# Moving SBUF blocks and reordering the routing of a one-core two-block forward pass

## The chip, the cores and the metric

The kernel runs on one core of one Trainium2 chip. The metric is the device time of one execution in microseconds; lower is better. A run of three executions gives a median with its lowest and highest value.

## The reference, cut to what matters

256 tokens of 1024 features go through two blocks in float32. The first block has two layers. Each layer is a hybrid mixer and a feed-forward; that of layer 0 is dense, that of layer 1 has eight experts of which each token takes two:

```python
def moe_swiglu(h, router_w, w1, w3, w2):
    t = h.reshape(bsz * seq, d)
    logits = jnp.einsum('td,de->te', t, router_w).astype(jnp.float32)
    top_vals, top_idx = lax.top_k(logits, TOP_K)          # TOP_K = 2
    top_w = jax.nn.softmax(top_vals, axis=-1)
    gates = jnp.sum(jax.nn.one_hot(top_idx, N_EXPERTS) * top_w[..., None], axis=1)
    for e in range(N_EXPERTS):
        a, b = t @ w1[e], t @ w3[e]
        out = out + gates[:, e:e + 1] * ((jax.nn.silu(a) * b) @ w2[e])
...
def second_block(x, ...):
    for l in range(DEPTH):                                # DEPTH = 2
        x = x + 0.5 * rmsnorm(swiglu_ffn(rmsnorm(x, g1), w_gu, w_down), g2)
        x = x + rmsnorm(mixing_sublayer(rmsnorm(x, g3), ..., rel_bias), g4)
        x = x + 0.5 * rmsnorm(swiglu_ffn(rmsnorm(x, g5), w_gu, w_down), g6)
```

The attention inside `mixing_sublayer` adds a bias from a table of 32 buckets by distance (`rel_bias`). The kernel makes that table of distances once, during the first block.

## The kernel before, in words

**Weights.** All weights come in 591 slabs of 128 x 2048 float32 (1 MB), in the order of use, through a ring of three slots. SyncE loads each slab into `raw` in two halves; ScalarE rounds a half to fp32r in `whi` (line 301); VectorE writes the remainder to `wlo` (line 737); TensorE then takes the slab. ScalarE and VectorE run two slabs ahead of TensorE. A slot of `raw` is loaded again once VectorE has done with it.

**Products.** Each product is three matmuls, in `slab` (lines 1306 to 1308): high activations with `whi`, high activations with `wlo`, low activations with `whi`. The activation block of 128 x 128 is the stationary operand and 512 weight columns are the moving one. The split activations have names by stage: `XH`/`XL` for all mixers and the up half of the feed-forwards over all 256 tokens, `GH`/`GL` for their down half; `XEH`/`XEL` and `GH_`/`GL_` for the same halves of the experts, which take one tile of 128 gathered tokens.

**Memory.** `memory` allocates in the order of its lines, from 16.1 KiB of each partition on. Before: `raw` 16 to 40 KiB, `whi` 40 to 64, `wlo` 64 to 88, `X` 88 to 96, `XN` 96 to 104, `XH` 104 to 112, `XL` 112 to 120, then small tables (`ident`, `small`, `pcols`), `region_b` from 122 (in it `mcum` 122 to 128, `LFH` and `LFL` 141 to 145), and `region_z` from 148 (in it `GH` 148 to 170, `GL` 170 to 192; or `GH_` 148 to 159, `GL_` 159 to 170, `XEH` 176 to 180, `XEL` 180 to 184, `PT` 185 to 186, `YH` and `YL` 186 to 194).

**Around the routing.** Every engine has its own written program, and semaphores order them. After the second mixer (`m1.out`) TensorE transposes `X` (line 1338), ScalarE and VectorE split it into `XH` and `XL` (lines 313, 314, 754, 755). TensorE makes the table of distances into four PSUM banks (line 1599), ScalarE copies it to `RB` (line 545), and Pool writes it to DRAM and reads it back with each row shifted (lines 1843, 1847). Then come 64 small matmuls for the router's logits (line 1608), a chain of small steps on VectorE that picks two experts per token, each waited for by the next (`step`), five counting matmuls (lines 1615 to 1619), the slot of each token (`slots`, line 977), and the gather of expert 0's tokens (line 1542). Expert e is `up` with 22 slabs, then `down` with 11; between them the result of expert e - 1 is scattered (lines 1551, 1552) and added to `X` (line 993). All work after that runs in the same way for the second block.

Of the kernel before, what the change touches and what calls it, by code (L numbers as in the profile page):

```python
# [58 lines left out]
class Tiles:  # L59
# [54 lines left out]
    def memory(self):  # L114
        self.raw = self.sb("raw", [P, RING, SLAB])
        self.whi = self.sb("whi", [P, RING, SLAB], F32R)
        self.wlo = self.sb("wlo", [P, RING, SLAB], F32R)
# [34 lines left out]
        n = 9 * SEG  # L152
        z = self.overlays("region_z", n, [("Z", [P, n], F32)], [
            ("GH", [P, FT, S], F32R), ("GL", [P, FT, S], F32R),
            ("SG", [P, 3, NT, S], F32), ("GN", [P, 3, NT, S], F32),
        ], [
            ("GH_", [P, FT, P], F32R), ("GL_", [P, FT, P], F32R),
            ("SG_", [P, 3, S], F32), ("GN_", [P, 3, S], F32),
            ("XEH", [P, KT, P], F32R), ("XEL", [P, KT, P], F32R),
            ("PM", [P, NT, P], F32),  # L160
            ("PT", [P, S], F32R),
            ("YH", [P, D], F32R), ("YL", [P, D], F32R),
            ("GB", [P, D], F32), ("RW", [P, KT, NE], F32), ("RWH", [P, KT, NE], F32R), ("RWL", [P, KT, NE], F32R),
            ("iota_", [P, P], F32), ("iota", [P, P], F32), ("ltri", [P, 3, P], F32), ("mo", [P, 512], F32),
        ], [
            ("Z2", [P, 12 * NT * CW], F32),
            ("HP", [P, 2, 30 + S], F32), ("CA", [P, 2, S], F32), ("CB", [P, 2, S], F32),
            ("QT", [P, 2, S], F32), ("KTT", [P, 2, S], F32), ("QI", [P, 2, S], F32),
            ("LG", [P, 4, S], F32), ("SCO", [P, 2, S], F32), ("WRK", [P, 2, S], F32), ("m8", [P, 16], F32),
        ])  # L170
        self.Z, self.GH, self.GL, self.SG, self.GN, self.GH_, self.GL_ = (z[n] for n in ("Z", "GH", "GL", "SG", "GN", "GH_", "GL_"))
        self.SG_, self.GN_, self.XEH, self.XEL, self.PM, self.PT, self.YH = (z[n] for n in ("SG_", "GN_", "XEH", "XEL", "PM", "PT", "YH"))
        self.YL, self.GB, self.RW, self.RWH, self.RWL, self.iota_, self.iota = (z[n] for n in ("YL", "GB", "RW", "RWH", "RWL", "iota_", "iota"))
        self.ltri, self.mo, self.Z2, self.HP, self.CA, self.CB, self.QT = (z[n] for n in ("ltri", "mo", "Z2", "HP", "CA", "CB", "QT"))
        self.KTT, self.QI, self.LG, self.SCO, self.WRK, self.m8 = (z[n] for n in ("KTT", "QI", "LG", "SCO", "WRK", "m8"))
# [110 lines left out]
class Scalar(Engine):  # L286
# [195 lines left out]
    def up(self, T, tiles, norm=None):  # L482

        for g in range(FF_GROUPS):
            self.hi(2)
            if 0 < g < FF_GROUPS - 1:
                self.turn(T, g - 1, tiles)
            elif g:
                self.turn(T, g - 1, tiles)
            self.gate(T, g, tiles, norm)  # L490

# [232 lines left out]
class Vector(Engine):  # L724
# [297 lines left out]
    def first_max(self, src, m, onehot, RI):  # L1022

        dve, k = self.eng, self.k
        A, TM = k.hot(1), k.mo[:, 292:294]
# [5 lines left out]
        self.step(dve.tensor_tensor(onehot, A, bc(TM), ALU.is_equal))  # L1031

    def moe(self):
# [10 lines left out]
        dve.wait_ge(*k.at("e.iota_"))  # L1044
        dve.tensor_copy(k.iota[:], k.iota_[:].bitcast(I32))
        dve.wait_ge(*k.at("e.rw"))
        self.step(dve.tensor_copy(k.RWH[:], k.RW[:]))
        dve.tensor_tensor(k.RWL[:], k.RW[:], k.RWH[:], ALU.subtract).then_inc(*k.up("dve_step", "e.rws"))
        rbt = k.bias_tmp[0:REL_BUCKETS, 0:4]
        rbb = k.bias_tmp[0:REL_BUCKETS, 4 + 2 * S:4 + 4 * S].rearrange("p (h l) -> p h l", h=4)  # L1050
        dve.wait_ge(*k.at("rbt"))
        dve.tensor_copy(rbb, rbt.rearrange("p (h o) -> p h o", o=1).broadcast_to([REL_BUCKETS, 4, P])).then_inc(*k.up("dve_step", "rbb"))
        LG, A, B, OH1, OH2, SEL, _, RI = (k.hot(i) for i in range(8))
        M1, M2, _, W1, W2 = (mo[:, 288 + 2 * i:290 + 2 * i] for i in range(5))
        bc = lambda a: a.rearrange("p (t o) -> p t o", o=1).broadcast_to([P, NT, NE])
        POS = mo[:, 160:178].rearrange("p (t e) -> p t e", e=NE + 1)
        GATE = mo[:, 180:198].rearrange("p (t e) -> p t e", e=NE + 1)
        POS2 = mo[:, 200:218].rearrange("p (t e) -> p t e", e=NE + 1)
        CNT, FLAG = mo[:, 220:228], mo[:, 230:231].bitcast(I32)
        tt, ts = dve.tensor_tensor, dve.tensor_scalar  # L1060
        dve.wait_ge(*k.at("e.lg"))
        for t in range(NT):
            self.step(ts(LG[:, t, :], ps[:, 6, t * NE:(t + 1) * NE], rs[:, t:t + 1], None, ALU.mult))
        for t in range(NT):
            self.step(ts(RI[:, t, :], k.iota[:, 0:NE], -1.0, float(NE), ALU.mult, ALU.add))
        self.first_max(LG, M1, OH1, RI)
        self.step(dve.scalar_tensor_tensor(out=B, in0=OH1, scalar=-BIG, in1=LG, op0=ALU.mult, op1=ALU.add))
        self.first_max(B, M2, OH2, RI)
        self.step(tt(W2, M2, M1, ALU.subtract), "e.w2")
# [209 lines left out]
    def program(self):  # L1279
# [16 lines left out]
class Tensor(Engine):  # L1296
# [247 lines left out]

    def scatter(self, T, e, t):
# [24 lines left out]
    def experts(self, T, GATE):  # L1570
# [4 lines left out]
        for e in range(NE):  # L1575
# [4 lines left out]
            self.up(U, 1, None, (lambda: self.scatter(T, e - 1, 0)) if e else None)  # L1580
# [10 lines left out]
    def moe(self):  # L1591
# [3 lines left out]
        rbb = k.bias_tmp[0:REL_BUCKETS, 4 + 2 * S:4 + 4 * S].rearrange("p (h l) -> p h l", h=4)  # L1595
# [15 lines left out]
        SEL, GATE = k.hot(5), mo[:, 180:198].rearrange("p (t e) -> p t e", e=NE + 1)  # L1611
        o = ps[:, 7, :]
# [6 lines left out]
        pe.matmul(o[:, 2 * NE:3 * NE], k.ltri[:, 1, :], SEL[:, 1, :], start=False, stop=True).then_inc(*k.up("pe_prod", "e.cum"))  # L1619
        pe.wait_ge(*k.at("e.flag"))  # L1620
        self.experts("x", GATE)
# [184 lines left out]
class Pool(Engine):  # L1806


    def start(self):
# [7 lines left out]
        pool.dma_start(k.mask_load[:], k.a["level_masks"]).then_inc(*k.up("d_mask_load", "mask_load", 16))  # L1817

# [229 lines left out]
```

## Time and profile before

| | |
|---|---|
| median of 3 executions | 3109.59 us (3104.79 to 3114.94) |
| the profiled execution, its own time | 3106.7 us |
| its span | 3104.9 us |
| TensorE (PE) busy | 2898.1 us, 93% |
| VectorE (DVE) busy | 2062.2 us, 66% |
| ScalarE (ACT) busy | 1696.0 us, 55% |
| DMA | 633.63 MB, mean 204 GB/s |
| experts, about 994 to 1823 us | DMA share 0.92 to 0.95 in each 100 us |

The span is the part of the time between the first and the last instruction in the profile. A busy share is an average over stages; matmuls overlap, so their busy time counts the stream of them and not each one's length. The granted clock is the share of 2.4 GHz that TensorE was given in a stretch; 0.5 is 1.2 GHz.

### The profile page before, as it was taken

The numbers are of one execution on the slowest core, as the hardware profiler recorded it, in microseconds if no ns is written. First come the engines' busy times: TensorE is split into PE (matmuls) and PEld (weight loads), VectorE is DVE, ScalarE is ACT, GpSimd is POOL, SyncE is SP. The second block draws the span as 40 slices with busy tenths as digits, with TensorE's granted clock in tenths as the row PEclk, the third lists the DMA queues.
The fourth block names the chain that finished last, engine by engine and source line by source line (L and its number), as shares of the span: only waits on it lengthen the run. The fifth ranks groups of instructions, "written<-read, shape, count | busy, mean of one in ns | idle before, by whom it ended". The sixth has DMA issues, their size and how long they took to land.

```text
span 3104.9 us, 34324 instructions
## 1 busy us (share of the span) xinstructions
PE 2898.1 (93%) x13334; PEld 2376.6 (77%) x13334; DVE 2062.2 (66%) x2910; ACT 1696.0 (55%) x2271; POOL 32.9 (1%) x55
## 2 busy tenths in 40 slices
PE   8998899999887999999999989989899999898998
PEld 6887688788765878777877768877778788776786
DVE  5566655656664898889888955468655455587553
ACT  5645354555523777677767754455454444555543
POOL 0000000000001000000000000000000000000000
PEclk9998899999987999999999989999999999999999
DMA  6443455454333999999989965544455555444453
GB/s 220 149 135 114 132 178 188 155 166 140 122 128 112 350 349 333 323 333 345 330 318 344 343 234 183 187 143 153 146 170 185 170 189 187 144 162 149 157 186 112
DMA packets 173658, 633.63 MB, mean 204 GB/s; under 512 B 19521, under 2 KB 19521, under 8 KB 173489
## 3 DMA queue, kind: packets, MB, share of 16 engines
q1 hardware_dynamic: 170752, 621.88, 59.0%
q0 software_dynamic: 2736, 9.49, 0.9%
q8 instruction: 107, 1.75, 0.2%
q14 instruction: 63, 0.51, 0.0%
HBM read 629.20 MB, written 2.10 MB: 203 GB/s over the span
## 4 chain that ended last, share of the span: by engine, by line
PE 78%; DVE 12%; DMA 4%; ACT 4%; issue 1%; SPq 0%; DVEq 0%; ACTq 0%; POOLq 0%
PE ps L1306 24%; PE ps L1308 23%; PE ps L1307 23%; DVE wlo L737 4%; DMA raw<-in_W 4%; PE ps L1418 2%; DVE CA L1182 2%; ACT whi L301 1%; PE ps L1495 1%; PE ps L1542 1%; PE ps L1338 1%; PE ps L1405 0%; PE ps L1404 0%; DVE XN L905 0%; DVE Z L1269 0%
## 5 line engine op out<-in xcount | busy, mean ns | idle before, releaser
L737 DVE TENSOR_TENSOR wlo<-raw,whi 128x1024 fp32r<-128x1024 f32 x1182 | 1394.0, 1221 | 560.4 <-ACT whi L301 550.8
L301 ACT ACTIVATE whi<-raw 128x1024 fp32r<-128x1024 f32 x1182 | 1197.8, 1057 | 600.8 <-PE ps L1308 547.7
L1306 PE MATMUL ps<-whi,XH 128*128 128x512 f32 (+1 forms) x2192 | 873.4, 398 | 41.2 <-DVE XL L755 17.3
L1307 PE MATMUL ps<-wlo,XH 128*128 128x512 f32 (+1 forms) x2192 | 859.0, 392 | 0.0
L1308 PE MATMUL ps<-whi,XL 128*128 128x512 f32 (+1 forms) x2192 | 859.0, 392 | 0.0
L1306 PEld LDWEIGHTS ps<-whi,XH 128*128 128x128 f32 x2192 | 418.8, 191 | 134.9 <-DVE XL L755 21.8
L1308 PEld LDWEIGHTS ps<-whi,XL 128*128 128x128 f32 x2192 | 417.6, 191 | 87.5
L1307 PEld LDWEIGHTS ps<-wlo,XH 128*128 128x128 f32 x2192 | 418.9, 191 | 82.8 <-issue 0.5
L1306 PE MATMUL ps<-whi,XEH 128*128 128x512 f32 x704 | 284.2, 404 | 1.4 <-DVE XEL L986 1.4
L1308 PE MATMUL ps<-whi,XEL 128*128 128x512 f32 x704 | 278.4, 395 | 0.0
L1307 PE MATMUL ps<-wlo,XEH 128*128 128x512 f32 x704 | 278.0, 395 | 0.0
L1306 PE MATMUL ps<-whi,GH 128*128 128x512 f32 x440 | 174.9, 397 | 0.0
L1308 PE MATMUL ps<-whi,GL 128*128 128x512 f32 x440 | 174.0, 395 | 0.0
L1307 PE MATMUL ps<-wlo,GH 128*128 128x512 f32 x440 | 174.0, 395 | 0.0
L1306 PE MATMUL ps<-whi,GH_ 128*128 128x512 f32 x352 | 147.8, 420 | 16.5 <-DVE X L993 16.5
L1308 PEld LDWEIGHTS ps<-whi,XEL 128*128 128x128 f32 x704 | 132.2, 188 | 31.6
L1306 PEld LDWEIGHTS ps<-whi,XEH 128*128 128x128 f32 x704 | 132.4, 188 | 30.0 <-DVE XEL L986 1.6
L1307 PEld LDWEIGHTS ps<-wlo,XEH 128*128 128x128 f32 x704 | 132.5, 188 | 28.7
L480 ACT ACTIVATE GH<-ps 128x512 fp32r<-128x512 f32 x55 | 32.9, 598 | 207.5 <-PE ps L1495 207.5
L943 DVE TENSOR_TENSOR GL<-ps,GH 128x512 fp32r<-128x512 f32 x55 | 38.0, 691 | 162.9 <-ACT GH L480 162.9
L1307 PE MATMUL ps<-wlo,GH_ 128*128 128x512 f32 x352 | 141.0, 400 | 0.0
L1308 PE MATMUL ps<-whi,GL_ 128*128 128x512 f32 x352 | 140.8, 400 | 0.0
(358 smaller groups left out, 2467.9 us busy)
## 6 DMA issues: line engine op xcount, KB each, us to landing
raw<-in_W SPq DMA_DIRECT2D x1182, 512.0 KB, 5.2
GP<-in_ffn_post_g POOLq DMA_DIRECT2D x4, 512.0 KB, 4.0
X<-in_x SPq DMA_DIRECT2D x1, 1024.0 KB, 5.0
skew<-RB POOLq DMA_DIRECT2D x4, 256.0 KB, 2.8
RB<-skew POOLq DMA_DIRECT2D x8, 128.0 KB, 2.5
GP<-in_mix_post_g POOLq DMA_DIRECT2D x2, 512.0 KB, 3.8
out<-X SPq DMA_DIRECT2D x1, 1024.0 KB, 4.0
mload<-in_cum_sums POOLq DMA_DIRECT2D x1, 768.0 KB, 8.5
```

The lines of the kernel that those rows point to most:

```text
L301: act.activation(k.whi[:, slot, part], k.raw[:, slot, part], ACT.Copy).then_inc(*k.up("act_hi"))
L480: act.activation(GH[:, 2 * g:2 * g + 2, :], src, ACT.Copy).then_inc(*k.up("act_split", f"{T}.gh{g}"))
L737: dve.tensor_tensor(k.wlo[:, slot, part], k.raw[:, slot, part], k.whi[:, slot, part], ALU.subtract).then_inc(*k.up("dve_lo"))
L943: dve.tensor_tensor(GL[:, 2 * g:2 * g + 2, :], src, GH[:, 2 * g:2 * g + 2, :], ALU.subtract).then_inc(*k.up("dve_split", f"{T}.gl{g}"))
L1182: x = dve.scalar_tensor_tensor(out=CA[:, c, :], in0=HP[:, c, j:j + S], scalar=dw(c, j), in1=CA[:, c, :], op0=ALU.mult, op1=ALU.add)
L1306: pe.matmul(ps, xh, k.whi[:, slot, cols], start=first, stop=False)
L1307: pe.matmul(ps, xh, k.wlo[:, slot, cols], start=False, stop=False)
L1308: mm = pe.matmul(ps, xl, k.whi[:, slot, cols], start=False, stop=last)
L1338: mm = pe.transpose(bank[:, i * S + t * P:i * S + (t + 1) * P], src(2 * b + i, t), k.ident[:])
L1418: mm = pe.matmul(o, x, x, start=True, stop=True)
L1495: mm = pe.transpose(turned[:, fb, t * P:(t + 1) * P], GN[:, t, fb * P:(fb + 1) * P], k.ident[:])
L1542: mm = pe.matmul(k.ps[:, 6 + c // 4, (c % 4) * P:(c % 4 + 1) * P], k.XN[:, t, c * P:(c + 1) * P], k.PM[:, t, :], start=t == 0, stop=t == N ...
```

## The change

Two things change. First the order of allocation. `wlo`, `ident`, `small`, `pcols` and the router's tables go to the end; `region_z` moves ahead of `region_b`. After: `raw` and `whi` as before, `X` 64 to 72 KiB, `XN` 72 to 80, `XH` 80 to 88, `XL` 88 to 96, `region_z` from 96 (`GH` 96 to 118, `GL` 118 to 140; `GH_` 96 to 107, `GL_` 107 to 118, `XEH` 124 to 128, `XEL` 128 to 132), `region_b` from 168, `wlo` 195 to 219.

Second the order of the routing. The router's tables are loaded at the start and prepared on VectorE behind the first mixer; the bias rows are copied behind the second mixer; the table of distances is made by TensorE and copied by ScalarE after the first two slabs of expert 0; the gates are worked out after the slots; two comparisons become one instruction each; the counts go to bank 5 and the unused ninth column of the slot tables goes away.

```diff
     def memory(self):
         self.raw = self.sb("raw", [P, RING, SLAB])
         self.whi = self.sb("whi", [P, RING, SLAB], F32R)
-        self.wlo = self.sb("wlo", [P, RING, SLAB], F32R)
         self.X = self.sb("X", [P, NT, D])
         self.XN = self.sb("XN", [P, NT, D])
         self.XH = self.sb("XH", [P, KT, S], F32R)
         self.XL = self.sb("XL", [P, KT, S], F32R)
-        self.ident = self.sb("ident", [P, P])
-        self.small = self.sb("small", [P, 192])
-        self.pcols = self.sb("pcols", [P, PCOLS])
-
+        n = 9 * SEG
+        z = self.overlays("region_z", n, [("Z", [P, n], F32)], [
...
         b = self.overlays("region_b", 6816, [
...
+        self.wlo = self.sb("wlo", [P, RING, SLAB], F32R)
+        self.ident = self.sb("ident", [P, P])
+        self.small = self.sb("small", [P, 192])
+        self.pcols = self.sb("pcols", [P, PCOLS])
...
+    def distances(self):
+        act, k = self.eng, self.k
+        act.wait_ge(*k.at("dist"))
+        act.activation(k.RB[:].rearrange("p t h l -> p (t h l)").rearrange("p (h l) -> p h l", h=4), k.ps[:, 4:8, :], ACT.Copy).then_inc(*k.up("act_step", "distc"))
+
...
-            self.up(U, 1)
+            self.up(U, 1, None, self.distances if U == "x.e0" else None)
...
     def moe(self):
         act, k = self.eng, self.k
         self.norm_in("e.n", lambda i: k.pcols[:, LCOLS + 8 + i:LCOLS + 9 + i])
-        act.wait_ge(*k.at("dist"))
-        act.activation(k.RB[:].rearrange("p t h l -> p (t h l)").rearrange("p (h l) -> p h l", h=4), k.ps[:, 4:8, :], ACT.Copy).then_inc(*k.up("act_step", "distc"))
         W2 = k.mo[:, 296:298]
...
+    def router_tables(self):
+        dve, k = self.eng, self.k
+        dve.wait_ge(*k.at("e.iota_"))
+        self.step(dve.tensor_copy(k.iota[:], k.iota_[:].bitcast(I32)))
+        dve.tensor_scalar(k.small[:, 144:152], k.iota[:, 0:NE], -1.0, float(NE), ALU.mult, ALU.add).then_inc(*k.up("dve_step"))
+        dve.wait_ge(*k.at("e.rw"))
+        self.step(dve.tensor_copy(k.RWH[:], k.RW[:]))
+        dve.tensor_tensor(k.RWL[:], k.RW[:], k.RWH[:], ALU.subtract).then_inc(*k.up("dve_step", "e.rws"))
...
-        self.step(dve.tensor_tensor(A, src, bc(m), ALU.is_equal))
-        self.step(dve.tensor_tensor(A, A, RI, ALU.mult))
+        for t in range(NT):
+            x = dve.scalar_tensor_tensor(out=A[:, t, :], in0=src[:, t, :], scalar=m[:, t:t + 1], in1=RI, op0=ALU.is_equal, op1=ALU.mult)
+        self.step(x)
...
         self.lo(LEAD)
         self.mixer1(0)
+        self.router_tables()
         self.ffn1()
         self.mixer1(1)
+        self.bias_rows()
         self.moe()
...
-            self.up(U, 1, None, (lambda: self.scatter(T, e - 1, 0)) if e else None)
+            self.up(U, 1, None, (lambda: self.scatter(T, e - 1, 0)) if e else self.distances if U == "x.e0" else None)
+            if U == "x.e0":
+                pe.wait_ge(*k.at("distc"))
...
+    def distances(self):
+        pe, k = self.eng, self.k
+        rbb = k.bias_tmp[0:REL_BUCKETS, 4 + 2 * S:4 + 4 * S].rearrange("p (h l) -> p h l", h=4)
+        pe.wait_ge(*k.at("rbb"))
+        pe.wait_ge(*k.at("hot"))
+        pe.wait_ge(*k.at("e.flag"))
+        for h in range(4):
+            mm = pe.matmul(k.ps[:, 4 + h, :], rbb[:, h, :], k.bias_tmp[0:REL_BUCKETS, 4:4 + 2 * S], start=True, stop=True)
+        mm.then_inc(*k.up("pe_prod", "dist"))
...
         self.norm_in("e.n", ["m1.out"])
-        rbb = k.bias_tmp[0:REL_BUCKETS, 4 + 2 * S:4 + 4 * S].rearrange("p (h l) -> p h l", h=4)
-        pe.wait_ge(*k.at("rbb"))
-        pe.wait_ge(*k.at("hot"))
-        for h in range(4):
-            mm = pe.matmul(ps[:, 4 + h, :], rbb[:, h, :], k.bias_tmp[0:REL_BUCKETS, 4:4 + 2 * S], start=True, stop=True)
-        mm.then_inc(*k.up("pe_prod", "dist"))
         pe.wait_ge(*k.at("e.n3.l"))
         pe.wait_ge(*k.at("e.rws"))
-        pe.wait_ge(*k.at("distc"))
```

TensorE's program behind the second mixer, before (`RWH` and `RWL` are the router's split weights, `bias_tmp` the rows of the table):

```order
L1308 MATMUL ps<-whi,XL 128x512
L1338 MATMUL ps<-ident,X 128x128 x16
L1599 MATMUL ps<-bias_tmp 128x512 x4
L1608 MATMUL ps<-RWH,XH 128x8
L1608 MATMUL ps<-RWL,XH 128x8
```

and after:

```order
L1323 MATMUL ps<-whi,XL 128x512
L1353 MATMUL ps<-ident,X 128x128 x16
L1630 MATMUL ps<-RWH,XH 128x8
L1630 MATMUL ps<-RWL,XH 128x8
L1630 MATMUL ps<-RWH,XL 128x8
```

The table's matmuls no longer stand between the transposes and the logits. They stand in expert 0 now, after its first two slabs:

```order
L1321 MATMUL ps<-whi,XEH 128x512
L1322 MATMUL ps<-wlo,XEH 128x512
L1323 MATMUL ps<-whi,XEL 128x512
L1569 MATMUL ps<-bias_tmp 128x512 x4
L1321 MATMUL ps<-whi,XEH 128x512
```

Here a slab's matmuls stand on both sides of them. VectorE's program from the second choice to the slots, before (`mo` holds all small routing values, `PM` the slots):

```order
L1069 TENSOR_TENSOR mo<-mo 128x2
L1071 TENSOR_SCALAR mo<-mo 128x2
L1072 RECIPROCAL mo<-mo 128x2
L1073 TENSOR_TENSOR mo<-mo 128x2
L1074 MEMSET mo 128x60
L1075 TENSOR_TENSOR mo<-mo 128x16
L1076 TENSOR_TENSOR mo<-mo 128x16
L1077 TENSOR_TENSOR mo<-mo 128x2x8
L1078 TENSOR_TENSOR mo<-mo 128x16
L1080 TENSOR_SCALAR mo<-ps 128x16
```

and after:

```order
L1079 TENSOR_TENSOR mo<-mo 128x16
L1080 TENSOR_TENSOR mo<-mo 128x2
L1083 SCALAR_TENSOR_TENSOR XN<-X,small,GB 128x1024 x2
L1086 TENSOR_SCALAR mo<-ps 128x16
L1087 TENSOR_TENSOR mo<-mo 128x16
L1088 TENSOR_SCALAR mo<-mo 128x16
L979 TENSOR_SCALAR PM<-iota,mo 128x128 x2
L1091 TENSOR_SCALAR mo<-mo 128x2
L1092 RECIPROCAL mo<-mo 128x2
```

The sum of the two choices (1078, now 1079), for which the counting matmuls wait, stands first; `XN` stands between it and the step that reads the counts; the gates stand behind the slots.

## Rows read from the trace of the kernel before

**Rows 1.** The page's head.
```profile
span 3104.9 us, 34324 instructions
```
**Rows 2.** The chain of waits around the routing: start, length, work.
```profile
951.38 2.48 DVE XN L1042 x2
...
954.74 7.21 PE ps L1599 x8
961.97 1.89 ACT RB L545
963.99 13.80 PE ps L1608 x64
...
983.17 0.60 PE ps L1615 x2
...
987.64 5.36 PE ps L1542 x32
...
994.40 0.50 PE ps L1306
```
**Rows 3.** TensorE's timeline, steady work of feed-forward 0: start, length, instruction.
```profile
480.08 0.39 PE L1306 MATMUL ps<-whi,XH 128*128 128x512 f32 x1
...
489.38 0.40 PE L1308 MATMUL ps<-whi,XL 128*128 128x512 f32 x1
...
555.16 0.40 PE L1306 MATMUL ps<-whi,GH 128*128 128x512 f32 x1
...
564.96 0.40 PE L1306 MATMUL ps<-whi,GH 128*128 128x512 f32 x1
```
**Rows 4.** VectorE's timeline in the routing.
```profile
948.07 0.47 DVE L755 SCALAR_TENSOR_TENSOR XL<-ps,pcols,XH 128x256 fp32r<-128x256 f32 x1
...
977.82 0.49 DVE L1063 TENSOR_SCALAR mo<-ps,small 128x8 f32<-128x8 f32 x2 [23.13 <-PE ps L1608]
...
982.94 0.17 DVE L1078 TENSOR_TENSOR mo<-mo 128x16 f32<-128x16 f32 x1
```
**Rows 5.** Stretches: length, busy us, then granted clock, DMA share, GB/s.
```profile
948.00:954.00 6.00, 0.00 (x0) 0.00 (x0) 3.32 (x7) 3.12 (x6) 0.00 (x0) 0.66 0.00 0
...
962.00:978.00 16.00, 13.79 (x64) 13.73 (x64) 0.18 (x1) 3.13 (x2) 6.41 (x12) 0.50 0.42 132
...
480.00:565.00 85.00, 85.00 (x379) 69.24 (x378) 42.02 (x44) 35.62 (x43) 0.00 (x0) 1.00 0.57 187
```
**Rows 6.** VectorE's timeline behind the first mixer.
```profile
386.54 0.48 DVE L754 SCALAR_TENSOR_TENSOR XL<-ps,pcols,XH 128x256 fp32r<-128x256 f32 x1 [1.62 <-ACT XH L314]
```
**Rows 7.** DMA issues of the table, 900 to 1060 us: size, us to landing.
```profile
skew<-RB POOLq DMA_DIRECT2D x4, 256.0 KB, 2.8
RB<-skew POOLq DMA_DIRECT2D x8, 128.0 KB, 2.5
```
**Rows 8.** Stretches inside the experts; columns as in rows 5.
```profile
1010.00:1040.00 30.00, 30.00 (x136) 24.16 (x135) 27.89 (x32) 24.41 (x32) 0.00 (x0) 1.00 1.00 364
...
1080.00:1180.00 100.00, 98.34 (x452) 79.71 (x452) 88.41 (x94) 74.02 (x91) 0.00 (x0) 1.00 0.95 336
```
**Rows 9.** TensorE's timeline, decay sums and a scatter.
```profile
103.27 0.39 PE L1404 MATMUL ps<-mcum,LFH 128*128 128x512 f32 x1
...
105.13 0.40 PE L1306 MATMUL ps<-whi,XH 128*128 128x512 f32 x1
...
1099.57 0.40 PE L1551 MATMUL ps<-YH,PT 128*128 128x512 f32 x1
...
1100.48 0.40 PE L1306 MATMUL ps<-whi,XEH 128*128 128x512 f32 x1
```
**Rows 10.** Groups of instructions on the page: busy, mean ns, idle before.
```profile
L301 ACT ACTIVATE whi<-raw 128x1024 fp32r<-128x1024 f32 x1182 | 1197.8, 1057 | 600.8 <-PE ps L1308 547.7
...
L1307 PE MATMUL ps<-wlo,XH 128*128 128x512 f32 (+1 forms) x2192 | 859.0, 392 | 0.0
...
L1306 PE MATMUL ps<-whi,GH_ 128*128 128x512 f32 x352 | 147.8, 420 | 16.5 <-DVE X L993 16.5
```

More of the change, by code:

```diff
@@ L121, in memory @@
         self.XL = self.sb("XL", [P, KT, S], F32R)
-        self.ident = self.sb("ident", [P, P])
-        self.small = self.sb("small", [P, 192])
-        self.pcols = self.sb("pcols", [P, PCOLS])
+        n = 9 * SEG
+        z = self.overlays("region_z", n, [("Z", [P, n], F32)], [
+            ("GH", [P, FT, S], F32R), ("GL", [P, FT, S], F32R),
+            ("SG", [P, 3, NT, S], F32), ("GN", [P, 3, NT, S], F32),
+        ], [
+            ("GH_", [P, FT, P], F32R), ("GL_", [P, FT, P], F32R),
+            ("SG_", [P, 3, S], F32), ("GN_", [P, 3, S], F32),
+            ("XEH", [P, KT, P], F32R), ("XEL", [P, KT, P], F32R),
+            ("PM", [P, NT, P], F32),
+            ("PT", [P, S], F32R),
+            ("YH", [P, D], F32R), ("YL", [P, D], F32R),
+            ("GB", [P, D], F32), ("mo", [P, 512], F32),
+        ], [
+            ("Z2", [P, 12 * NT * CW], F32),
+            ("HP", [P, 2, 30 + S], F32), ("CA", [P, 2, S], F32), ("CB", [P, 2, S], F32),
+            ("QT", [P, 2, S], F32), ("KTT", [P, 2, S], F32), ("QI", [P, 2, S], F32),
+            ("LG", [P, 4, S], F32), ("SCO", [P, 2, S], F32), ("WRK", [P, 2, S], F32), ("m8", [P, 16], F32),
+        ])
+        self.Z, self.GH, self.GL, self.SG, self.GN, self.GH_, self.GL_ = (z[n] for n in ("Z", "GH", "GL", "SG", "GN", "GH_", "GL_"))
+        self.SG_, self.GN_, self.XEH, self.XEL, self.PM, self.PT, self.YH = (z[n] for n in ("SG_", "GN_", "XEH", "XEL", "PM", "PT", "YH"))
+        self.YL, self.GB, self.mo, self.Z2, self.HP, self.CA, self.CB, self.QT = (z[n] for n in ("YL", "GB", "mo", "Z2", "HP", "CA", "CB", "QT"))
+        self.KTT, self.QI, self.LG, self.SCO, self.WRK, self.m8 = (z[n] for n in ("KTT", "QI", "LG", "SCO", "WRK", "m8"))
         b = self.overlays("region_b", 6816, [
@@ L150, in memory @@
         self.gvb, self.ones, self.ones1, self.mask_load, self.GP, self.bias_tmp = (b[n] for n in ("gvb", "ones", "ones1", "mask_load", "GP", "bias_tmp"))
[L152 to L174, printed above, removed]
@@ L175, in memory @@
-        self.KTT, self.QI, self.LG, self.SCO, self.WRK, self.m8 = (z[n] for n in ("KTT", "QI", "LG", "SCO", "WRK", "m8"))
+        self.wlo = self.sb("wlo", [P, RING, SLAB], F32R)
+        self.ident = self.sb("ident", [P, P])
+        self.small = self.sb("small", [P, 192])
+        self.pcols = self.sb("pcols", [P, PCOLS])
+        self.RW, self.RWH, self.RWL = self.sb("RW", [P, KT, NE]), self.sb("RWH", [P, KT, NE], F32R), self.sb("RWL", [P, KT, NE], F32R)
+        self.iota_, self.iota, self.ltri = self.sb("iota_", [P, P]), self.sb("iota", [P, P]), self.sb("ltri", [P, 3, P])
@@ L480, in turn, with up @@
         act.activation(GH[:, 2 * g:2 * g + 2, :], src, ACT.Copy).then_inc(*k.up("act_split", f"{T}.gh{g}"))
-    def up(self, T, tiles, norm=None):
+    def up(self, T, tiles, norm=None, after_first=None):
         for g in range(FF_GROUPS):
             self.hi(2)
-            if 0 < g < FF_GROUPS - 1:
-                self.turn(T, g - 1, tiles)
-            elif g:
+            if g:
                 self.turn(T, g - 1, tiles)
             self.gate(T, g, tiles, norm)
+            if g == 0 and after_first:
+                after_first()
     def down(self, T, tiles, between=None):
@@ L1038, in moe @@
         self.norm_in("e.n", lambda i: k.pcols[:, LCOLS + 8 + i:LCOLS + 9 + i])
-        dve.wait_ge(*k.at("e.n.rs"))
+        LG, A, B, OH1, OH2, SEL = (k.hot(i) for i in range(6))
+        M1, M2, _, W1, W2 = (mo[:, 288 + 2 * i:290 + 2 * i] for i in range(5))
+        bc = lambda a: a.rearrange("p (t o) -> p t o", o=1).broadcast_to([P, NT, NE])
+        POS = mo[:, 160:176].rearrange("p (t e) -> p t e", e=NE)
+        GATE = mo[:, 180:196].rearrange("p (t e) -> p t e", e=NE)
+        POS2 = mo[:, 200:216].rearrange("p (t e) -> p t e", e=NE)
+        CNT, FLAG = mo[:, 220:228], mo[:, 230:231].bitcast(I32)
+        tt, ts = dve.tensor_tensor, dve.tensor_scalar
+        dve.wait_ge(*k.at("e.n.rs"))
+        dve.wait_ge(*k.at("e.lg"))
+        for t in range(NT):
+            x = ts(LG[:, t, :], ps[:, 6, t * NE:(t + 1) * NE], rs[:, t:t + 1], None, ALU.mult)
+        self.step(x)
+        self.first_max(LG, M1, OH1)
+        self.step(dve.scalar_tensor_tensor(out=B, in0=OH1, scalar=-BIG, in1=LG, op0=ALU.mult, op1=ALU.add))
+        self.first_max(B, M2, OH2)
+        self.step(tt(SEL, OH1, OH2, ALU.add), "e.sel")
+        self.step(tt(W2, M2, M1, ALU.subtract), "e.w2")
         dve.wait_ge(*k.at("e.gb"))
@@ L1043, in moe @@
         x.then_inc(*k.up("dve_step", "e.xn"))
[L1044 to L1049, printed above, removed]
-        rbb = k.bias_tmp[0:REL_BUCKETS, 4 + 2 * S:4 + 4 * S].rearrange("p (h l) -> p h l", h=4)
[L1051 to L1069, printed above, removed]
+        dve.wait_ge(*k.at("e.cum"))
+        self.step(ts(A, ps[:, 5, 0:16].rearrange("p (t e) -> p t e", t=NT), 1.0, None, ALU.add))
+        self.step(tt(A, A, SEL, ALU.mult))
+        self.step(ts(POS, A, -1.0, None, ALU.add))
+        self.slots("x", 0, POS)
         dve.wait_ge(*k.at("e.w2e"))
@@ L1619, in moe @@
         pe.matmul(o[:, 2 * NE:3 * NE], k.ltri[:, 1, :], SEL[:, 1, :], start=False, stop=True).then_inc(*k.up("pe_prod", "e.cum"))
+        self.experts("x", GATE)
         pe.wait_ge(*k.at("e.flag"))
-        self.experts("x", GATE)
         more = pe.value_load(mo[0:1, 230:231].bitcast(I32), min_val=0, max_val=1)
```

41 lines of the change are left out of this document (20 added, 21 removed).

## The prediction

> **What bounds the kernel now.** I read the page first, for the span of 3104.9 us [rows 1] and for who is busy, then stretches of it: in feed-forward 0 TensorE is busy 85.00 of 85 us [rows 5], in the experts 98.34 of 100 us [rows 8]. So the time is TensorE's own work and the few places where it stops. Then the chain of waits at the place that the diff touches. Between the second mixer's last output and the first expert's first weight slab lies a stretch with no weight work: transposes of X, the distance table at 954.74, its copy on ScalarE at 961.97, the router's 64 small matmuls at 963.99, the counting matmuls at 983.17, the gather at 987.64, the first slab at 994.40 [rows 2]. These are a chain, each step waiting for the one before, and the weight ring holds only three slabs, so the DMA stands still too. Third, the distance between starts of neighbouring matmuls in steady work. With stationary XH or XL it is (489.38 - 480.08) / 41 = 0.2268 us, with GH or GL it is (564.96 - 555.16) / 42 = 0.2333 us [rows 3]. Both are 512 columns at the full clock (1.00 from 480 to 565 [rows 5]) and share whi and wlo as moving operand. What differs is where the stationary block lies: XH and XL at 104 to 120 KiB, GH and GL at 148 to 192 KiB.
>
> **The change, part by part: the routing.** (a) The table leaves the way. Now the router's matmuls wait for its copy; later they wait only for XL, whose last piece starts at 948.07 and takes 0.47 [rows 4], so they can start at 948.54 instead of 963.99: 15.4 us less. XN, iota and the split of the router's weights also stood ahead of the table's product on VectorE, from 951.38 on; the split and iota are done long before in the new order, and XN comes later (d). (b) The 64 matmuls took 13.8 us at the half clock, 1.2 GHz: the granted clock was 0.66 between 948 and 954, where no matmul ran, and 0.50 from 962 to 978 [rows 5]. In the new order they start during that fall, so the first few may run at 2.4 GHz; if all did, half of 13.8, 6.9 us, would go. In their 13.8 us at 1.2 GHz they did not raise the clock, so I take 0.7. (c) VectorE's steps from the logits (977.82) to the sum of the two choices (its last step at 982.94, 0.17 long) are 5.3 us; a step costs about 0.2 [rows 4]. Up to that sum the new order has 14 instructions in 11 waited steps, hence 11 x 0.2 and three more of 0.17, 2.7 us: 2.6 less. (d) From there to the gather it was 987.64 - 983.11 = 4.5 us. The counting matmuls (2.4) stay. XN (2.48 for the pair [rows 2]) now runs beside them, with one small step ahead, and ends some 0.3 later than they do. Behind it stand three steps and the slot pair instead of seven and the pair: 3.9 us, 0.6 less. The gates follow while the gather runs (5.4 us against nine steps, 1.9). Sum: 15.4 + 0.7 + 2.6 + 0.6 = 19.3 us less; bounds 17 (the steps save less than I count) and 25.5 (all 64 matmuls at the full clock).
>
> The tables now made on VectorE right behind the first mixer are four short instructions, under 1 us; there it idled 1.62 us for ScalarE's first XH piece [rows 6]; the next step would be 1 us late only if that cover went. The 0.4 us copy of the bias rows stands in the same kind of gap behind the second mixer. Pool's loads move to the start, ahead of bias_tmp, which is wanted 900 us later. No cost.
>
> **The table inside expert 0.** TensorE does the same eight passes, 7.2 us at the half clock [rows 2], so 3.6 at the full one. The experts have no slack for them: there TensorE has 1.7 us of 100 to spare [rows 8]. ScalarE waits in line for the table and copies it (1.89 us) before it splits the next slab; two slabs are split ahead, 5.6 us of TensorE's work, against 1.9 + 2 x 1.06 [rows 10] and VectorE's half about as long again, 5.1, so that just fits. Behind the copy Pool writes four blocks of 256 KB and reads eight of 128 KB [rows 7], 2.1 MB. They ran in the idle stretch; now they meet the weights where the DMA share is 1.00 at 364 GB/s [rows 8]: 2.1 / 0.364 = 5.8 us of transfer. Bounds: 3.6 us (transfers hidden, TensorE being late anyway) and 3.6 + 5.8 = 9.4. The DMA runs just in time there and the two delays overlap, so I take 6.5.
>
> **The addresses.** As allocated, whi stays at 40 to 64 KiB. wlo goes from 64 to 88 up to 195 to 219, XH and XL from 104 to 120 down to 80 to 96. GH takes 96 to 118 and GL 118 to 140. In the experts GH_ and GL_ take 96 to 118, XEH 124 to 128, XEL 128 to 132 (before: 148 to 184). Nothing in the trace shows a wlo this high beside a low stationary block. The nearest rows: the scatter has both operands high (PT 185, YH and YL 186 to 194), and its starts lie (1100.48 - 1099.57) / 4 = 0.2275 apart [rows 9], as close as with both low. So a high stationary block alone is not what costs 7 ns; a pair of which one is low and one high is. The decay sums of the first mixer, with LFH and LFL at 141 to 145 and mcum at 122 to 128, go at (105.13 - 103.27) / 8 = 0.2325 [rows 9], which says that a boundary lies near 120 to 140, where GL and XEL will stand. By the pair reading, three matmuls (whi with XH, wlo with XH, whi with XL) take 0.680 now and 0.687 with wlo high.
> - XH and XL: 2192 such threes [rows 10] x 6.7 ns = 14.6 us more; TensorE waits for others in small parts of the mixers, so 13.
> - GH and GL: 5 feed-forwards x 11 slabs x 8 = 440 threes at 0.700. With half of GL beyond the boundary they come to about 0.687: 6 us less.
> - Experts: 704 threes with XEH and 352 with GH_, now 0.700 (the 352 are counted in rows 10; 8 experts x 22 slabs x 4 are the 704). XEL, high, is loaded while wlo, high, streams, so 20 ns less on the 704 and 13 on the 352: 18.8 us. But the DMA share there is already 0.95 at 336 GB/s [rows 8], and TensorE's waits for X before the down slabs (16.5 us in all [rows 10]) have VectorE behind them, queued for late slabs. I take half, 9; bounds 4 and 19.
>
> Where the rows give one number, the Trainium skill gives another: "SBUF — State Buffer", section "Who interferes with whom", says that TensorE never waits on anyone and names no address as slow. By it the address part is worth nothing, while rows 3 differ by 7 ns between blocks that differ in nothing else. I go by the rows; the rule's outcome is the third rival.
>
> **Sum**: -19.3 + 6.5 + 13 - 6 - 9 = -14.8 us. The profiled execution took 3106.7 us, so 3091.9; it lies 2.9 below the median of the three runs, 3109.6, and against that median the forecast is 3094.8, rounded to 3095.
>
> **Rivals.** (1) Only the stationary address counts, wlo's does not. For it: every slow three above has a high stationary block, and I have just one kind of row with both high. Against it: that row. Then XH and XL cost nothing, GH and GL save 7 us, the experts 704 x 13.3 ns + 352 x 20 ns = 16.4 us, of which 9 come through: -19.3 + 6.5 - 7 - 9 = -29, 3081. (2) The slower side: wlo high costs at both changes, from whi to wlo and from wlo back, 13.3 ns per XH three. For it: a switch to a far moving operand is not shown free anywhere. That is 29 us, 26 of them felt; GH keeps 2 and the experts 4, so +26 - 6 - 12.8 = +7, 3117. It decides from about 8 ns per XH three on (12.8 + 6 = 18.8 us over 2192). (3) The addresses do nothing, the 7 ns has another cause, and only the routing is left: -19.3 + 6.5 = -12.8, 3097. For it: the page's rule; against it: rows 3.
>
> **Chances.** Forecast 0.40, (1) 0.30, (2) 0.15, (3) 0.15. A measurement here can tell about 0.3%, 9.3 us, from no change. The forecast's own range is 3082 to 3106, from routing 17 to 25, table 3.6 to 9.4 and experts 4 to 19. Faster than 3100.3: 0.8 of the forecast, all of (1), 0.75 of (3), 0.1 of (2), together 0.75; within the bound 0.15; slower 0.10. The range goes from (1) with more of the experts' gain and part of the clock's (3070) to (2) at 3117, cut at 3116.
>
> **What would show it.** The first router matmul at about 5 us behind the last X, still at or near the full clock; the gather's start 19 us earlier; the table's eight passes behind the first two slabs of expert 0 and the Pool transfers inside a stretch with DMA share 1.00. Then the starts in steady work: XH threes at 0.687 (forecast), 0.680 (rivals 1 and 3) or 0.693 (rival 2); GH threes at 0.687, or still 0.700 (rival 3). And experts that each take about 1 us less, expert 0 apart. The prediction is wrong if the XH threes stay at 0.680, which makes it faster, or if expert 0 loses more than the upper bound because the weights fall behind for good.

## The result: slower by 0.4%, not faster by 0.5%

Over 12 runs of each on the same chips the kernel before took 3112.89 us (median) and the changed one 3122.61 us: ratio 1.0038, 95% interval 1.0027 to 1.0049. The forecast was 3095 against 3109.6, a ratio of 0.9953; the time lies above the whole range, on the slower side. The profiled execution of the changed kernel took 3126.1 us against the 3106.7 us that the sum was made for: 19.4 more instead of 14.8 less. One execution each of two kernels below took 14.8 and 7.2 ms; it is in their medians and not in their ratios, which compare undisturbed executions alone.

The page of the changed kernel, its head and one group (columns as in [rows 10]):

```profile
span 3124.1 us, 34321 instructions
...
L1322 PE MATMUL ps<-wlo,XH 128*128 128x512 f32 (+1 forms) x2192 | 868.2, 396 | 0.0
```

Against [rows 10] the wlo-with-XH group's mean went from 392 to 396 ns. The matmuls' ends are modelled, so the distance between starts says more. TensorE's timeline of the changed kernel in the feed-forward of [rows 3]:

```profile
479.88 0.40 PE L1321 MATMUL ps<-whi,XH 128*128 128x512 f32 x1
...
481.98 0.40 PE L1321 MATMUL ps<-whi,XH 128*128 128x512 f32 x1
...
554.82 0.40 PE L1321 MATMUL ps<-whi,GH 128*128 128x512 f32 x1
...
560.42 0.40 PE L1321 MATMUL ps<-whi,GH 128*128 128x512 f32 x1
```

A "three" is the group of three matmuls that makes one product. Three threes with XH take 2.10 us, 0.700 each (0.680 before), and eight with GH 5.60, again 0.700. XH was to go to 0.687, GH down to 0.687.

The chain of waits around the routing (start, length, work), as [rows 2]:

```profile
952.41 1.24 DVE X L925
...
958.53 13.83 PE ps L1630 x64
972.46 0.37 DVE mo L1074 x2
...
975.50 2.48 DVE XN L1083 x2
978.52 0.49 DVE PM L979 x2
979.05 6.67 PE ps L1557 x32
...
987.12 0.50 PE ps L1321
...
992.94 3.64 PE ps L1569 x8
...
1007.05 9.85 DMA raw<-in_W
```

The router's matmuls (L1630) follow 4.9 us behind the last X and the gather (L1557) 25.4 behind it; before, the gather came 43.95 behind (987.64 against a last X that ended at 943.69). The table (L1569) has gone into expert 0, and behind it stands one long wait for a weight load.

With the ends of VectorE's X updates as marks (for expert 0 the first of its two), the difference of the two profiled executions (after minus before, us) splits so:

| stretch | before | after | difference | forecast |
|---|---|---|---|---|
| start to the end of mixer 2 | 943.7 | 953.6 | +9.9 | part of the +13 - 6 |
| to the first slab of expert 0 | 50.7 | 33.5 | -17.2 | -19.3 |
| to the X update of expert 0 | 108.2 | 115.1 | +6.9 | +6.5 |
| experts 1 to 7 | 722.5 | 728.4 | +6.0 | -9 |
| to the last X update of the kernel | 1275.4 | 1289.1 | +13.7 | rest of the +13 - 6 |

Routing and expert 0 did nearly what was forecast. Of the error of some 34 us, 32 are in the three rows of the addresses: +29.6 instead of -2. The other 2.5 are in the routing and expert 0.

### The profile page after: what moved, and what is told of

Read it like the earlier page. It is cut to its first block, busy times and chain, and to the rows that moved or that the text cites. A ratio compares the mean times of both kernels' runs of the same rounds, so it can differ in the third digit from the quotient of the medians.

```text
span 3124.1 us, 34321 instructions
## 1 busy us (share of the span) xinstructions
PE 2924.0 (94%) x13334; PEld 2376.5 (76%) x13334; DVE 2061.2 (66%) x2907; ACT 1696.2 (54%) x2271; POOL 33.4 (1%) x55
## 4 chain that ended last, share of the span: by engine, by line
PE 74%; DVE 14%; DMA 7%; ACT 4%; issue 1%; SPq 0%; DVEq 0%; ACTq 0%; POOLq 0%
PE ps L1321 22%; PE ps L1322 22%; PE ps L1323 22%; DMA raw<-in_W 7%; DVE wlo L739 7%; PE ps L1433 2%; DVE CA L1195 2%; ACT whi L300 1%; PE ps L1557 1%; PE ps L1510 1%; PE ps L1353 1%; PE ps L1420 0%; PE ps L1419 0%; DVE XN L907 0%; DVE Z L1282 0%
## 5 line engine op out<-in xcount | busy, mean ns | idle before, releaser
L1321 PE MATMUL ps<-whi,XH 128*128 128x512 f32 (+1 forms) x2192 | 883.9, 403 | 42.2 <-DVE XL L757 19.9
L1322 PE MATMUL ps<-wlo,XH 128*128 128x512 f32 (+1 forms) x2192 | 868.2, 396 | 0.0
```

Source lines behind the costliest of these rows:

```text
L1321: pe.matmul(ps, xh, k.whi[:, slot, cols], start=first, stop=False)
L1322: pe.matmul(ps, xh, k.wlo[:, slot, cols], start=False, stop=False)
```

## The experiments

In every kernel below the length of a three is the time from one matmul of whi with XH (or GH) to the next such matmul; the means are over all unbroken threes of the trace (1867 to 1875 with XH, 420 with GH).

**Routing alone, layout alone, wlo back, XH last.** The first keeps the old places with the new routing, the second the new places with the old routing. The third is the changed kernel with one tensor moved, the fourth the kernel before with XH and XL behind everything.

```diff
 # wlo third (from the changed kernel)
+        self.wlo = self.sb("wlo", [P, RING, SLAB], F32R)   # behind whi
-        self.wlo = self.sb("wlo", [P, RING, SLAB], F32R)   # behind region_b
 # XH last (from the kernel before): the two lines below go behind region_z
-        self.XH = self.sb("XH", [P, KT, S], F32R)
-        self.XL = self.sb("XL", [P, KT, S], F32R)
```

> The new order of the routing with the old places of all blocks (router tables added at the end). Theory A (the routing gains, the addresses lose): 10 to 13 us faster than before, since the changed kernel's stretch from the last X of the second mixer to expert 0's X add is 10.4 us shorter; XH threes stay at 0.680, GH threes at 0.700. Rival B (the moved table spoils the later experts for good): within 4 us of before, because what is gained ahead of expert 0 is lost again in experts 1 to 7.

Measured: 3093.39 us, ratio 0.9947 (0.9932 to 0.9962); XH 0.681, GH 0.700. That is 16 us, on the side of more than the 12.8 worked out.

> The new places of all blocks with the old order of the routing. Theory A: 20 to 25 us slower than before, with XH threes at 0.700 nearly everywhere and GH threes still at 0.700. Rival B: 8 to 12 us slower, all of the measured loss.

Measured: 3135.79 us, ratio 1.0083 (1.0067 to 1.0099), 26 us slower; XH 0.697, GH 0.700. So the layout alone costs more than the whole change, and costs it at XH.

> The changed kernel with wlo back in its old third place, all else behind it by 24 KiB (XH 104 to 112, XL 112 to 120, GH 120 to 142, GL 142 to 164). Theory A1 (a high wlo slows the threes): XH threes 0.680 again, 24 to 30 us faster than the changed kernel, so 10 to 15 faster than before; GH threes somewhere from 0.687 to 0.700. Rival A2 (XH and XL were worse at 80 to 96 KiB than at 104 to 120): the same here, to be told apart by a kernel with both low.

Measured: 3084.14 us, ratio 0.9915 (0.9892 to 0.9938); XH 0.6815, GH 0.681. One tensor's place is worth 1.0038 against 0.9915, about 38 us.

> The kernel before with XH and XL allocated last (204 to 220 KiB), wlo low. If a high stationary block beside low moving operands costs 20 ns a three, the XH threes come to 0.700 and the time to 25 to 40 us above before. If only wlo's place counts, XH threes stay at 0.680 and the time within 5 us.

Measured in one execution: 3146.02 us; XH and GH both 0.700. The XH threes of all four kernels can still be told by height: a pair of a low and a high operand is slow. But GH at 120 to 164 KiB in the third kernel gave 0.681, and GH at 132 to 176 in the fourth 0.700; height alone does not order these two. What does is the start address as a remainder. `pcols` takes 416 bytes (392, rounded up to a multiple of 32) and region_b 27,264, neither a multiple of 256, so whatever stands behind one of them is shifted. The blocks that a matmul reads lie multiples of 512 bytes behind the start of their tensor, so the start alone sets the remainder. From the allocation of each kernel, the start address modulo 256 bytes:

| kernel | whi | wlo | XH, XL | GH, GL | XH three | GH three |
|---|---|---|---|---|---|---|
| before; routing alone | 128 | 128 | 128 | 160 | 0.681 | 0.700 |
| changed; layout alone | 128 | 0 | 128 | 128 | 0.697 | 0.700 |
| wlo third | 128 | 128 | 128 | 128 | 0.6815 | 0.681 |
| XH last | 128 | 128 | 160 | 160 | 0.700 | 0.700 |

A three is at 0.680 where all its operands agree and near 0.700 where one does not. The scatter and the decay sums of [rows 9] fit as well: mcum leaves 32 and LFH 160 (0.2325 a matmul), PT, YH and YL all 160 (0.2275). This table was read off after the runs, so it had to be put to the test against height.

**High but agreeing; GH shifted in place.** The first is the changed kernel with wlo exchanged with region_b: wlo at 168.1 KiB, remainder 128. The second is the kernel before with 224 unused bytes.

```diff
 # wlo high and agreeing (from the changed kernel): wlo's line goes ahead of region_b
+        self.wlo = self.sb("wlo", [P, RING, SLAB], F32R)
         b = self.overlays("region_b", 6816, [
 # the kernel before, region_z shifted
+        self.sb("shift", [P, 56])
         n = 9 * SEG
         z = self.overlays("region_z", n, [("Z", [P, n], F32)], [
```

> The changed kernel with wlo exchanged with region_b: wlo still lies high, at 168.1 KiB behind region_z instead of 194.75, but its start address now leaves 128 modulo 512 bytes as whi, XH, XL and region_z do (256 before). Theory H, height (a low/high pair of operands is spaced wider): XH and XL stay low, so XH threes stay near 0.693 to 0.700 us and the time stays within 5 us of the changed kernel's, near 3120. Theory M, modulo (the spacing depends on whether the start addresses of the operands agree in their remainder): XH threes 0.680, GH threes 0.680, the time near that of the kernel with wlo back in third place, ratio 0.991 to 0.993 to the kernel before, some 30 us under the changed kernel.

Measured: 3083.14 us, ratio 0.9907 (0.9887 to 0.9927); XH 0.681, GH 0.681. TensorE's timeline of that kernel:

```profile
481.46 0.39 PE L1321 MATMUL ps<-whi,XH 128*128 128x512 f32 x1
...
486.90 0.39 PE L1321 MATMUL ps<-whi,XH 128*128 128x512 f32 x1
```

Eight threes in 5.44 us, 0.680 each, with wlo still 88 KiB above XH. Height is out as the cause.

> The kernel before with 224 unused bytes ahead of region_z and nothing else: GH and GL stay at 148.6 and 170.6 KiB, but their remainder modulo 512 goes from 416 to 128, that of whi and wlo. Theory H, height: GH threes stay at 0.700 us, ratio 1.000. Theory M, modulo: GH threes 0.680, some 450 threes by 0.020 us = 9 us, ratio 0.997; XH threes 0.680 by both. Experts 1 to 7 stay at 725 to 730 us by both if their bound is the transfers.

Measured: 3094.26 us, ratio 0.9953 (0.9936 to 0.9971); GH 0.6805. Its timeline where [rows 3] have 0.2333 a matmul:

```profile
554.24 0.39 PE L1307 MATMUL ps<-whi,GH 128*128 128x512 f32 x1
...
559.68 0.39 PE L1307 MATMUL ps<-whi,GH 128*128 128x512 f32 x1
```

5.44 / 8 = 0.680. 224 bytes that nobody uses made the kernel before about 14.6 us faster. In the profiled executions, 18.3 us apart, the five feed-forwards are 1.0 to 1.6 us shorter each, 7.0 together, where 9 were worked out from the threes; the four mixers, parts of which use region_z too, give 6.4, routing with expert 0 1.2 and the other experts 3.7. What the mixers gave was not forecast and not taken apart.

**Which differences cost.** The kernel before with 8 or 32 floats of padding ahead of XH and padding ahead of region_z.

```diff
+        self.sb("shx", [P, 8])      # 32 in the second kernel
         self.XH = self.sb("XH", [P, KT, S], F32R)
...
+        self.sb("shz", [P, 64])     # 88 in the second kernel
         n = 9 * SEG
```

> The kernel before with 32 unused bytes ahead of XH (remainder modulo 512: 160 against the 128 of whi and wlo) and padding ahead of region_z so that GH and GL have 192 (a difference of 64). Theory H: XH threes 0.680 and GH 0.700, as in the kernel before. Theory M: which difference costs is open; a difference of 32 modulo 256 cost 0.020 us in the kernel before (GH) and in the one with XH last, so XH threes 0.700 are expected, some 2,190 by 0.020 = 40 us; GH at a difference of 64 between 0.680 and 0.700.

Measured in one execution: 3147.84 us; XH 0.700, GH 0.700. XH, lower than GH and at its old height but for 32 bytes, now costs as much as the old GH.

> The kernel before with 128 unused bytes ahead of XH (a difference of 128 from whi and wlo) and padding ahead of region_z so that GH and GL differ from whi and wlo by 256. Theory H: XH threes 0.680, GH 0.700. Theory M: in the changed kernel wlo differed by 128 and XH threes took 0.693, so XH near 0.693 to 0.700 here; GH 0.680 if the remainder counts modulo 256, 0.700 if modulo 512.

Measured in one execution: 3126.76 us; XH 0.6985, GH 0.681. From its timeline:

```profile
480.02 0.39 PE L1308 MATMUL ps<-whi,XH 128*128 128x512 f32 x1
...
482.12 0.40 PE L1308 MATMUL ps<-whi,XH 128*128 128x512 f32 x1
...
554.76 0.39 PE L1308 MATMUL ps<-whi,GH 128*128 128x512 f32 x1
...
560.20 0.39 PE L1308 MATMUL ps<-whi,GH 128*128 128x512 f32 x1
```

2.10 / 3 = 0.700 and 5.44 / 8 = 0.680. A difference of 128 costs and one of 256 does not: it is the remainder modulo 256 that must agree. Differences of 32, 64 and 128 cost nearly the same.

**Any common remainder; one odd operand.** The first is the kernel before with whi, wlo, XH and XL last, so that all of them and GH leave 160 (whi 156, wlo 180, XH 204, XL 212 KiB). The second shifts XL alone by 32 bytes and pads region_z to 128.

```diff
+        self.sb("shl", [P, 8])
         self.XL = self.sb("XL", [P, KT, S], F32R)
...
+        self.sb("shz", [P, 48])
         n = 9 * SEG
```

> The kernel before with whi, wlo, XH and XL last (156 to 220 KiB) and region_z in the middle; start addresses of all five leave 416 modulo 512 (160 modulo 256), raw, X and XN 128. Theory M (only agreement of the matmul's operands counts, neither their height nor the remainder itself): all threes 0.680, time like that of the kernel before with the shifted region_z, ratio near 0.995. Theory M128 (128 modulo 256 is the good remainder): all threes 0.700, 40 us or more over the kernel before.

Measured in one execution: 3102.86 us beside 3114.71 for the kernel before; XH 0.681, GH 0.680. From its timeline:

```profile
480.18 0.39 PE L1304 MATMUL ps<-whi,XH 128*128 128x512 f32 x1
...
485.62 0.39 PE L1304 MATMUL ps<-whi,XH 128*128 128x512 f32 x1
```

Again eight threes in 5.44 us. With whi, wlo, XH and XL at 156 to 220 KiB and GH and GL at 84 to 128, height plays no part, and 160 serves as well as 128: only agreement counts.

> The kernel before with 32 unused bytes ahead of XL alone (XL leaves 160 modulo 256; XH, whi and wlo 128) and region_z padded to 128. If each matmul pays by its own two operands, only the third matmul of a three is wider: 0.2267, 0.2267, 0.2333, a three 0.687. If the cost is that of the next stationary block being loaded while a moving block streams, only the second is wider, 0.687 too. If one odd operand disturbs all three: 0.700. GH threes 0.680 by each.

Measured in one execution: 3124.38 us; XH 0.699, GH 0.6805. Its timeline:

```profile
479.98 0.40 PE L1308 MATMUL ps<-whi,XH 128*128 128x512 f32 x1
480.21 0.40 PE L1309 MATMUL ps<-wlo,XH 128*128 128x512 f32 x1
480.45 0.39 PE L1310 MATMUL ps<-whi,XL 128*128 128x512 f32 x1
480.68 0.40 PE L1308 MATMUL ps<-whi,XH 128*128 128x512 f32 x1
```

The three starts lie 0.23, 0.24 and 0.23 apart (means over all: 0.2324, 0.2385, 0.2285): the odd operand is in one matmul of three, and all three are wider than in the kernel before (0.2272, 0.2270, 0.2269), the last by little. In the changed kernel, where wlo is the odd one, the means are 0.2336, 0.2331 and 0.2302. Neither simple rule of a pair paying by itself holds; how the one operand reaches its neighbours stays open. The middle gap, in which wlo streams and XL is next to be loaded, is the widest, which is a hint and no more.

**What bounds the experts.** Two kernels in which the loads of the experts' slabs bring three quarters of each half, so that the rest of the weights is stale.

```diff
+                if MOE_BASE + RING <= base + self.n < MOE_BASE + NE * FF_SLABS:
+                    part = slice(h * HALF, h * HALF + 3 * HALF // 4)
                 sp.dma_start(k.raw[:, slot, part], k.a["W"][base + self.n, :, part]).then_inc(k.of(f"land{slot}{h}"), 16)
```

> The changed kernel with wlo back in third place (threes at 0.680), and in the experts' slabs each load brings only the first three quarters of its half slab; the rest of the half keeps what an earlier slab left there, so the experts' weights are not the reference's. Instructions of all compute engines are the same. Theory T (experts 1 to 7 are bound by the weight transfers, share 0.94): with 0.75 of the bytes they go from 728 us to 695 to 712, TensorE's own work. Rival C (they are bound by the compute engines' order): within 5 us of 728.

> The changed kernel with the same short loads in the experts and the same weights wrong (wlo differs in its remainder, threes near 0.695 to 0.700). Theory T: once the transfers no longer bound them, the experts show the wider spacing, 7 experts by 132 threes by 0.013 to 0.020 us = 12 to 18 us more than in the same kernel with wlo third. Rival C: the difference between the two stays under 3 us, as without the short loads (731 against 728).

Measured in one execution each: 3053.44 and 3104.53 us. From the X update of expert 0 to the last one the first took 700.3 us (727.1 with full loads), the second 707.6 (728.4). A window inside the experts (columns as in [rows 5]) of the changed kernel, with full loads:

```profile
1180.00:1280.00 100.00, 97.03 (x440) 78.62 (x439) 85.49 (x93) 73.08 (x91) 0.00 (x0) 0.98 0.92 331
```

and of the first kernel with short loads, wlo third:

```profile
1180.00:1280.00 100.00, 98.43 (x463) 81.32 (x462) 88.51 (x96) 73.88 (x94) 0.00 (x0) 1.00 0.75 259
```

463 matmuls in 100 us instead of 440, at a DMA share of 0.75 instead of 0.92: with a quarter less to fetch the experts run 21 to 27 us faster, so it is the transfers that hold them. And the spacing shows again: 700.3 against 707.6, 7.3 us, where full loads left 1.3. In all fourteen profiled executions with full loads this stretch took 717.7 to 733.0 us, and both 717.7 and 730.7 came with XEH threes at 0.683 to 0.684; there the spacing can't be read off it: the eight with XEH threes at 0.683 to 0.685 average 724.5 us, the six with 0.695 to 0.700 average 727.0. Theory T holds in kind; its 12 to 18 us were too many, since the changed kernel's threes in the experts are at 0.695, not 0.700 (7 x 132 x 0.011 = 10).

**The table behind the last expert.** The kernel with wlo third, once more as a partner, and with the distance table taken out of expert 0:

```diff
 # TensorE, end of moe
+        pe.wait_ge(*k.at("x.end_dve"))
+        self.distances()
 # TensorE and ScalarE, expert 0
-            self.up(U, 1, None, self.distances if U == "x.e0" else None)
+            self.up(U, 1)
 # feed-forward behind the experts
-        self.ff2("g10", ["fin.out", "rb"])
+        self.ff2("g10", ["fin.out"], ["distc"])
```

> The kernel with wlo back in third place once more, as the partner of the next one on the same chip: ratio 0.990 to 0.993 to the kernel before.

Measured: 3088.29 us, ratio 0.9928 (0.9910 to 0.9947), as the first time within the intervals.

> The kernel with wlo back in third place, with the four matmuls of the distance table, their copy and the eight plus four transfers taken out of expert 0 and put behind the last expert, where TensorE waits some 12 us for the final norm. Theory: expert 0 gives back what it lost, 6.5 to 7 us (148.5 to 142 up to its X add), and 0 to 2 us come back behind the last expert: 5 to 7 us under its partner. Rival: the stall in expert 0 came from weight transfers that are late anyway, and the experts' transfers take up the gain: within 2 us of its partner. Rival 2: the copy and the table's bulk delay the final norm: more than its partner.

Measured: 3082.55 us, ratio 0.9901 (0.9879 to 0.9924), 5.7 us under its partner's median (6.7 by the median of its five other executions, without the one of 7.2 ms); the two intervals overlap, so the order of the two is likely and not shown by the times alone. In the stages, the stretch from the end of mixer 2 to expert 0's X update took 141.1 us against 146.4, 5.3 less (148.5 in the first run of the partner). The chain behind the last expert:

```profile
1802.87 4.48 issue
1807.35 7.17 PE ps L1569 x8
...
1818.90 0.79 PE ps L1321
```

The eight passes run here at a granted clock of 0.50, 1.2 GHz (7.17 us; 3.64 inside the expert), behind 4.5 us of "issue". In TensorE's program the reading of the flag that says whether the experts need a second pass stands there; that it is what takes the 4.5 us is read from the order and not shown. The whole is longer than the gap: the first slab comes 16.0 us behind the last X update, against 13.5. So 2.6 us come back, a part of rival 2, and the two places that the edit touches give 2.7 net against this run of the partner. The profiled execution's span is 8.6 us shorter; 5.3 of that lie in experts 1 to 7 (721.8 against 727.1), inside the scatter of that stretch. The time fits the theory's 5 to 7, but by the stages the move itself gains less. Its ratio is the lowest of the kernels with complete weights, though not clear of the 0.9907 of wlo high and agreeing.

## Why the prediction was wrong, step by step

- **Routing, -19.3: right**, with -18.5 at the gather. (a) The logits start 15.4 us nearer to the last X, as worked out. (b) The 64 matmuls took 13.83 us against 13.80: the clock's 0.7 did not come; in the other kernels with the new order they took 13.5 to 13.8. (c) From the logits (972.36) to the sum of the two choices 2.9 us, forecast 2.7. (d) To the gather 3.8, forecast 3.9. Not counted: the gather took 6.67 us instead of 5.36, which leaves -17.2 at the first slab. That is the chance of one execution and no price of the new order: in the seven other kernels with that order the gather took 5.2 to 5.8 (last section).
- **The table inside expert 0, +6.5: right**, with +6.9. Its passes took 3.64 us (3.6 forecast). The price came the way described: TensorE waited behind a weight load of 9.85 us. With the table behind the experts the longest load in the chain at this place took 6.90, so 3.64 + 2.95 = 6.6 is worked out, close to the 6.9. The table taken out again gave back 5.3 us against one run of the partner and 7.4 against the other.
- **The addresses: the failed step.** It is the pair reading, "a pair of which one is low and one high is" what costs 7 ns. The rows that it stood on were right, but height was the wrong thing to sort them by; the remainder of the start addresses modulo 256 sorts them too, and only it survives the kernels with wlo high and agreeing, GH shifted by 224 bytes, and everything high. The prediction took the addresses from the allocation in whole KiB and so could not see it.
  - XH and XL: +13 forecast by 0.687 a three; 0.697 measured, 16 ns by 2192 = 34 us worked out, against +9.9 and +13.7, together 24, in the stretches outside routing and experts. Those stretches hold all else that moving the blocks did too: 224 bytes ahead of region_z alone made the four mixers 6.4 us shorter. The parts were not taken apart.
  - GH and GL: -6 forecast; 0 measured. region_z had come to agree with whi, but wlo no longer did: 0.700 for another reason than before.
  - Experts: -9 forecast by halving 18.8; +6.0 measured. Two things failed here. The 18.8 took 20 and 13 ns off a three, by the same pair reading; measured were 4 (0.699 to 0.695), worth 1056 x 4 ns = 4 us. And the halving was too kind: with the loads at a DMA share of 0.91 to 0.96 next to nothing of a closer spacing comes through (wlo third had 0.684 and 726.0 and 727.1 us, the kernel before 0.699 and 722.5). The +6.0 itself lies inside the scatter of full-load executions.
- **The rivals.** (2) came nearest in time (3117) and in the XH spacing (0.693), and its threshold, 8 ns per three, was passed; but its mechanism, a high wlo, is refuted by the kernel with wlo high and agreeing, so that it came near is luck. (1) and (3) needed XH at 0.680. Rival (3) was the outcome of the Trainium skill's "SBUF — State Buffer", section "Who interferes with whom", where TensorE never waits on anyone. In this case the same matmuls come every 0.2267 or every 0.2333 us by the start address of an operand alone. No run says whether that is a wait on SBUF or another cost inside TensorE, so the page's sentence is neither confirmed nor refuted, but it can't be used to price an address at nothing.
- **The range.** The bounds that the prediction names for its own case (routing 17 to 25, table 3.6 to 9.4, experts 4 to 19) add up to 3076 to 3105 and not to 3082 to 3106. None of this reaches the measured time; XH and XL, the part that failed, had no bounds of their own.
- **The chances.** 0.10 for slower was too little: both costs named for a layout change were prices of one unknown, and three of the four cases let the unknown be cheap.

## What to carry over

Before moving a tensor that TensorE reads, list the byte addresses of the matmul's operands modulo 256, not their places in KiB; a small tensor of odd size ahead of a large one shifts everything behind it, and some unused bytes put it right. Compare the distance between matmul starts of groups that should be alike: a difference of 3% between two groups of one kernel was a gain of 0.5% waiting for 224 bytes. And credit a stage that its transfers bound with nothing for faster compute; cut the bytes in a trial to see which it is.

## What the runs showed of the hardware

- 512-column matmuls in steady work start every 0.2267 us when the start addresses of stationary and moving operands agree modulo 256 bytes, and every 0.232 to 0.2333 when one operand differs by 32, 64 or 128 bytes, at the full granted clock and at any height in SBUF between 40 and 220 KiB. Differences under 32 bytes weren't tried.
- One odd operand in a rotation of three matmuls widens all three (0.2324, 0.2385, 0.2285).
- The gather's 32 matmuls took 6.67 us in the changed kernel and 5.36 before, with the same instructions. The new order is not the reason. The kernel with short loads and wlo last is the changed kernel up to there, and its gather, as far behind the last X (25.4 us), took 5.25. The same window in the changed kernel

```profile
979.00:986.00 7.00, 6.66 (x32) 6.47 (x32) 2.11 (x10) 0.85 (x2) 0.00 (x0) 0.57 0.00 0
```

and in that one

```profile
979.00:986.00 7.00, 5.34 (x33) 5.15 (x33) 3.00 (x12) 2.07 (x4) 0.00 (x0) 0.77 0.00 0
```

show the difference: the mean granted clock was 0.57 in one and 0.77 in the other. Over all kernels the gather took 5.2 to 6.7 us with the new order and 5.3 to 6.7 with the old one. When the full clock comes back varies from one execution to the next, and more than 1 us hangs on it here.
